# A two-layer encoder trunk on one core: the layer loop is written out in every engine's program, and the router's logits are computed in four column groups

## The reference

```python
xn = rms_norm(x, norm1_w[l])
cols = xn @ w_in[l]
attn = mla_branch(...)        # low-rank attention, 16 heads
hy = hyena_branch(...)        # gated long convolutions, by a transform
merged = gates[:, :, 0] * (attn @ w_attn_branch[l]) + gates[:, :, 1] * (hy @ w_hyena_branch[l])
x = x + merged @ w_out[l]
x = x + expert_choice_ffn(rms_norm(x, norm2_w[l]), router_w[l], ...)
```

```python
def expert_choice_ffn(h, router_w, wg, wu, wd):
    C = max(1, EC_CAPACITY_FACTOR * S // N_EXPERTS)              # 32
    aff = jax.nn.softmax((h @ router_w).astype(jnp.float32), axis=-1)
    gate, idx = lax.top_k(jnp.swapaxes(aff, 1, 2), C)            # 32 tokens for each of 16 experts
    ...                                                          # xs: the tokens of each expert
    a = jnp.einsum('becd,edf->becf', xs, wg)
    u = jnp.einsum('becd,edf->becf', xs, wu)
    o = jnp.einsum('becf,efd->becd', jax.nn.silu(a) * u, wd) * gate[..., None]
    ...                                                          # added back to their tokens
```

## Time and profile before

| | us |
|---|---|
| median of three executions | 2113.52 |
| lowest and highest | 2112.22, 2116.02 |
| the profiled execution | 2112.32 |
| span of the profiled execution, first to last instruction | 2110.5 |
| PE busy | 1606.2 (76%) |
| DVE busy | 508.7 (24%) |
| ACT busy | 287.6 (14%) |
| DMA, mean over the span | 305 GB/s read |

### The profile page before, as it was taken

One profiled execution on the slowest core, in us unless ns is written; L12 is line 12 of the kernel. 1 busy time (PEld: TensorE's weight loads), 2 busy tenths in 40 slices (PEclk: granted clock), 3 DMA queues, 4 the chain that ended last, 5 costly groups with the idle time before them and its releaser, 6 DMA issues.

```text
span 2110.5 us, 23405 instructions
## 1 busy us (share of the span) xinstructions
PE 1606.2 (76%) x9552; PEld 909.9 (43%) x9552; DVE 508.7 (24%) x1057; ACT 287.6 (14%) x594; POOL 45.7 (2%) x24
## 2 busy tenths in 40 slices
PE   7999999876466566666689999997865665665665
PEld 4687688432232132232256866884322222321322
DVE  2654541111111111111126545402111111111111
ACT  2233200200000000000022332002000000000000
POOL 0300000000000000000002000000000000000000
PEclk9999999988788888878899999999887887888888
DMA  7522024679999999999945220246899999999997
GB/s 282 195 85 100 1 80 190 245 319 430 435 423 430 430 427 430 432 429 426 426 149 199 80 100 1 80 189 258 341 434 426 426 430 434 423 430 430 427 430 319
DMA packets 36352, 644.83 MB, mean 306 GB/s; under 512 B 3984, under 2 KB 4880, under 8 KB 6160
## 3 DMA queue, kind: packets, MB, share of 16 engines
q1 hardware_dynamic: 35472, 638.84, 72.2%
q10 hardware_dynamic: 768, 4.29, 0.7%
HBM read 642.07 MB, written 1.05 MB: 305 GB/s over the span
## 4 chain that ended last, share of the span: by engine, by line
PE 49%; DMA 42%; issue 4%; DVE 3%; DVEq 1%; SPq 1%; ACT 1%; ACTq 0%
DMA region<-w_down_dram 27%; DMA ring<-w_up_dram 15%; PE ps L695 7%; PE ps L394 7%; PE ps L619 5%; PE ps L461 5%; PE ps L719 3%; PE ps L644 3%; PE ps L552 2%; PE ps L681 2%; PE ps L587 2%; PE ps L577 2%; PE ps L422 2%; PE ps L484 1%; PE ps L439 1%
## 5 line engine op out<-in xcount | busy, mean ns | idle before, releaser
L695 PE MATMUL ps<-ring,uT 128*32 128x384 f32 (+1 forms) x4096 | 437.7, 567 | 296.8 <-DMA ring<-w_gate_dram 147.6
L695 PEld LDWEIGHTS ps<-ring,uT 128*32 128x32 f32 x4096 | 182.9, 130 | 550.6 <-issue 205.6
L719 PE MATMUL ps<-region,uT 128*32 128x512 f32 x1408 | 175.8, 596 | 34.9 <-DVE uT L1266 22.2
L1262 DVE TENSOR_TENSOR uT<-uT,ps 128x256 f32<-128x256 f32 x32 | 13.5, 421 | 699.4 <-PE ps L695 699.4
L394 PE MATMUL ps<-xnT,ring 128*128 128x256 f32 x768 | 178.3, 380 | 4.5 <-DVE uT L942 2.9
L394 PEld LDWEIGHTS ps<-xnT,ring 128*128 128x128 f32 x768 | 140.6, 190 | 24.1 <-DVE uT L942 4.5
L734 PE MATMUL ps<-uT 128*128 128x512 f32 x256 | 124.3, 618 | 28.8 <-ACT uT L926 28.8
L920 ACT ACT_TABLE_LOAD x32 | 41.1, 1283 | 631.3 <-PE ps L695 631.3
L461 PE MATMUL ps<-xnT,ring 128*128 128x256 f32 x512 | 115.0, 380 | 0.0
L719 PEld LDWEIGHTS ps<-region,uT 128*32 128x32 f32 x1408 | 44.5, 109 | 143.9 <-issue 105.3
L1273 DVE TENSOR_TENSOR x<-x,ps 128x512 f32<-128x512 f32 x128 | 87.9, 687 | 64.4 <-PE ps L734 64.4
(11 more groups left out here) (195 smaller groups left out, 1368.1 us busy)
## 6 DMA issues: line engine op xcount, KB each, us to landing
ring<-w_gate_dram SPq DMA_DIRECT2D x64, 2816.0 KB, 28.4
ring<-w_up_dram SPq DMA_DIRECT2D x32, 5632.0 KB, 32.8
region<-w_down_dram SPq DMA_DIRECT2D x64, 2048.0 KB, 30.6
ring<-units_dram SPq DMA_DIRECT2D x34, 2048.0 KB, 8.0
region<-w_down_dram SPq DMA_DIRECT2D x32, 1536.0 KB, 37.2
ring<-w_lat_dram SPq DMA_DIRECT2D x4, 1344.0 KB, 20.6
ring<-w_q_b_dram SPq DMA_DIRECT2D x2, 2304.0 KB, 29.1
region<-filt_dram ACTq DMA_DIRECT2D x4, 512.0 KB, 11.9
```

The source lines that it names most:

```text
L695: m = mm(bank(b, QW[j], rows=CAP, row0=CAP * j), xs[:, i, q * CAP:(q + 1) * CAP], w[:, i, j * FT:j * FT + QW[j]], start=i == 0, stop=i == ...
L719: m = mm(bank(c, rows=CAP, row0=CAP * j), hT[:, b * P + CAP * j:b * P + CAP * (j + 1)], wd[:, CT * b + j, c * 512:(c + 1) * 512], start=b ...
```

## The change

1. `with engine.Fori(0, DEPTH) as L` becomes `for L in range(DEPTH)` on all five engines. The code of a layer now stands twice in each program, `L` is a number when the program is built, and the branch back to the first layer's code is gone. The inner loops stay.
2. The router's weights are padded from 16 to 32 columns for each block. Products 0 to 3 go to partitions 0, 32, 64 and 96 of bank 4, and products 4 to 7 are added to them in the same places. DVE then copies 128 rows in place of 16, and in place of the two transposes PE multiplies with a constant of 128 x 16 that holds a one where the row's number modulo 32 is the column: this transposes and adds the four groups at once.
3. The constants get 16 columns more (1057 KB become 1065 KB) and the layer's small parameters 128 (68 KB become 132 KB). An argument that makes a reserved scratch area smaller leaves the room for them. No transfer uses that area.

```diff
-W_N = DB + DB * E
+EP = 32
+W_N = DB + DB * EP
...
-        lgT = uT_t[0:E, 4096:4096 + S]
+        lgT = uT_t[:, 4096:4096 + S]
...
-            with sp.Fori(0, DEPTH) as L:
+            for L in range(DEPTH):
...
-            with pe.Fori(0, DEPTH) as L:
+            for L in range(DEPTH):
...
-                    m = mm(bank(4, S, rows=E), fvec[:, W_RT + i * E:W_RT + (i + 1) * E], aT[:, i],
-                           start=i == 0, stop=i == DB - 1)
+                    m = mm(bank(4, S, rows=EP, row0=EP * (i % 4)), fvec[:, W_RT + i * EP:W_RT + (i + 1) * EP], aT[:, i],
+                           start=i < 4, stop=i >= 4)
                 m.then_inc(s["lgT_psum"], 1)
...
-                    m = tp(bank(5, E, t * E), lgT[:, t * P:(t + 1) * P], ident[0:E, 0:E])
+                    m = mm(bank(5, E, t * E), lgT[:, t * P:(t + 1) * P], cst[:, C_SUM:C_SUM + E], start=True, stop=True)
...
-                copy(lgT, bank(4, S, rows=E)).then_inc(s["lgT_dve"], 1)
+                copy(lgT, bank(4, S)).then_inc(s["lgT_dve"], 1)
...
+    c[:, C_SUM:C_SUM + E] = np.arange(P)[:, None] % EP == np.arange(E)[None]
...
+    router = np.pad(k_major(a["router_w"]), ((0, 0), (0, 0), (0, 0), (0, EP - E)))
...
-    nc = bacc.Bacc("TRN2", target_bir_lowering=False, num_devices=1)
+    nc = bacc.Bacc("TRN2", target_bir_lowering=False, num_devices=1, dynamic_dma_scratch_size=2048)
```

More of the change, by code:

```diff
@@ L75 @@
 C_EPS = C_FEAT + S
-C_N = C_EPS + 1
+C_SUM = C_EPS + 1
+C_N = C_SUM + E
 KSC = QR + KVR
@@ L311, in _ @@
         def _(pool):
-            with pool.Fori(0, DEPTH) as L:
+            for L in range(DEPTH):
                 pool.wait_ge(s["qkw_scaled"], L + 1)
@@ L756, in _ @@
                 act.sem_inc(s[n], FREE)
-            with act.Fori(0, DEPTH) as L:
+            for L in range(DEPTH):
                 load_sqrt_table()
@@ L976, in _ @@
             dve.sem_inc(s["x_dve"], X_FREE)
-            with dve.Fori(0, DEPTH) as L:
+            for L in range(DEPTH):
                 dve.wait_ge(s["norm1_rms"], L + 1)
@@ L1337 @@
                            cols(a["filt_skip"].reshape(DEPTH, -1)), small], 2)
-    fvecs = np.concatenate([cols(a["norm2_w"]), k_major(a["router_w"]).reshape(DEPTH, P, -1)], 2)
+    router = np.pad(k_major(a["router_w"]), ((0, 0), (0, 0), (0, 0), (0, EP - E)))
+    fvecs = np.concatenate([cols(a["norm2_w"]), router.reshape(DEPTH, P, -1)], 2)
     qkw = np.concatenate([a["q_norm_w"], a["k_norm_w"]], 1)
```

## The result

The changed kernel takes 2096.7 us (median of six runs, 2094.92 to 2099.73) where the kernel before took 2112.87 us beside it (2109.29 to 2116.02). The ratio is 0.9926, with a 95% interval of 0.9915 to 0.9937: 16 us or 0.7% less. The forecast was 2107.7 us with 2103.8 to 2111.2 us; it was right in the direction and more than 7 us short at the nearer end. The profiled execution took 2094.92 us, its span is 2093.1 us, 17.4 us shorter than before.

The account below looks back on a forecast made before the run. The experts' weight stream sets the pace, so only savings before expert 1's first load count, once per layer. 2.6 + 2.8 + 0.2 + 0.2 = 5.8 us off 2112.32 gave 2106.5, as median 2107.7 us; range 2103.8 to 2111.2.

Parts of the forecast that it names:

- What bounds the kernel: Whole layer: time saved before expert 1's first gate load comes off the end; time saved after it is hidden by DMA.
- The router: Router's products, copy and sum in each layer: exponent 1.37 us sooner, taken as 1.3 us per layer, 2.6 us in all.
- DVE's gap: Second layer's start, L980: DVE waits for instructions after the layer loop's branch back; writing it out saves 2.8 us once.
- the first rival: Second layer's start: DVE's stall stays because code is fetched only when asked for; 2110.5 us, no measurable change; chance 0.16.
- the one with ACT's stalls: ACT's program, fetched piece by piece, stalls some 5.2 us each; two stalls give 2118.1 us, slower; chance 0.06.
- Registers: ACT's three transfers before the second layer's sum: without register instructions between them, 0.2 us off once (0 to 0.3).
- the other 0.2 us: Register work in other places, done while engines wait or have queued work: 0.2 us for the rest, between 0 and 2.
- The 10.8 us of fetching at each branch back of PE: PE's loop over expert groups: 10.8 us of instruction fetching at each branch back stay, hidden by a DMA share of 1.00.
- a DMA share below 1.00: Sign: a share below 1.00 from expert 1 on would make the reading of what is hidden fall.
- The other one: Sign that the forecast is right: time from expert 1's first load to the layer's end is unchanged.
- The third rival: Second layer's first transform products, 7.11 against 5.42 us: small shifts avoid half clock, 1.7 us more gained, 2105.6 us; chance 0.08.

## Why the prediction was right in part and wrong in the sum

**What bounds the kernel** was read rightly: what came sooner ahead of expert 1's gate load came off the end, and the run with PE late by 11 us in the stream shows that PE has room behind it.

**The router**, 2.6 us: right in the profile, where it gave 0.6 and 1.9 us and not 1.3 twice, and near it by medians. The second four products start 1.53 us after the first (forecast 1.54). They and the sum take 0.64 and 0.59 us, not 0.49 and 0.48, so the exponent comes 3.88 us after the first product and not 3.61; what follows made that up, and the gather is 1.37 us sooner, as forecast. PE's granted clock took some back in the first layer, where the gather's products needed 6.72 us at 0.55 on average (before 6.03 us at 0.61), and gave some in the second (5.47 us at 0.69, before 6.19 us at 0.60). By medians the router's part is 2.2 us with both loops at slot 0; with the layer loops kept it was at most 1.9 us.

**DVE's gap**, 2.8 us: right, both ways. It went from 2.84 to 0.03 us, and came back as 2.86 us with DVE's loop alone. The second layer did not pay for instructions behind full queues, so the first rival is out; so is the one with ACT's stalls, of which no run has any. **Registers**, 0.2 us: right. ACT's wait ahead of the second layer's sum is 3.29 us and was 3.45. For the other 0.2 us no run shows anything.

**"The 10.8 us of fetching at each branch back of PE stay, and are hidden: the DMA share over that stretch is 1.00."** This is the step that failed, twice. They don't stay: whether the loop is fetched anew depends on where its head lies (94 packets from slot 224, 40 from slot 0), and the layer loop written out moved the head. And they are not hidden. It is true that PE's standing still is hidden (11 us of it in a group left the streams at 568.70 and 568.78 us), but not the traffic. A DMA share of 1.00 says that the engines are taken, and in these runs further packets in that stretch were a cost and not free: 0.30 to 0.46 MB took 3.0 to 4.5 us of a stream. The prediction said that a DMA share below 1.00 would show this reading wrong; it read 1.01, so that sign could not have shown it. The other one, that the time from expert 1's load on is unchanged, did: 573.65 became 568.75 us. By the runs with the place alone this term is 8 to 10 us: 0.996 of before in one direction (8.4 us), 0.9926 against 0.9973 in the other (9.9 us).

**The third rival**, half the clock at the second layer's first transform products, came true beside the forecast. PE's granted clock was 0.50 from 1253.5 to 1255 us before, and is 1.00 over all of these products now. The changed kernel needs 5.42 us there, not 7.11:

```profile
1242.62 5.42 PE L554 MATMUL ps<-work,consts 128*128 128x512 f32 x12 [0.73 <-DVE work L1110]
```

The wait ahead of it is shorter because the decay table, for which DVE waits, is in use 4.9 us after its issue and not 6.0. In the eight cases with the layer loops kept (four runs, two layers each) that takes 5.5 to 6.2 us, in 23 of the 28 with them written out 4.8 to 5.0, in the other five 5.1 to 6.3. With DVE's gap, 2.8 us, these, 1.1 and 1.7 us, make up the 5.5 us between the streams of this pair of profiles. They are not in every run: where the loops were kept, the half clock came in the second layer once, in the first twice and once in neither, and it came once with them written out (the run with GpSimd's loop, first layer). So for the layer loop DVE's gap and the sum by medians are shown, the division of the rest is not. I had given the half clock a chance of 0.08 as an alternative; it was no alternative but a further term. The run with the loop's place alone and the one with the layer loop and slot 0 too (2103.5 and 2098.1 us, on two chips) differ by 5.4 us, much the same.

The sum as the runs have it: place 8.4, layer loop 5.4, router 2.2, together 16.0 us. The terms come from runs on different chips and are good to a microsecond or two.

Three things stay open: why 0.46 MB of further traffic costs 3 to 5 us of the stream and not 1.1, why fetching the loop anew once (9 packets) and twice (18) costs the first stream 3.0 and 3.2 us but three times only 4.9, and what in the layer loops makes the decay table land later, mostly by 0.9 us. No run puts back the loop of any engine but DVE, so it is not known which one's it is.

## What to carry to other kernels

The stage with a DMA share of 1.00 hid what an engine did (PE 11 us late in a group, streams unchanged), not what the DMA did (0.46 MB more, 3.0 to 4.5 us): count every packet in such a stage, those of the instruction queues too. Before and after any edit ahead of a long loop compare the packets of each instruction queue; if they jump, or gaps marked "issue" stand at the branch back, put the loop's head on the start of a block (96 packets became 42 here) or give its branch a hint (41) before judging the edit. And if a change moves such a loop, measure the change with the loop's place held, as the router could only be told with both at slot 0.

## What the runs showed of the hardware

- A loop of some 1600 PE instructions cost 96 or 94 packets of 16 KB at one place and 39 to 42 at another, in the same kernel. Each time that it was fetched anew PE stood still for 6.5 to 12.0 us.
- At a place between, the same program was fetched anew in some executions only: 2094 or 2100 to 2103 us, 57 packets in the profile of the slower kind and 39 in one of the faster. By the count in blocks of 256 instructions (259 to a packet in the run with the groups written out), the loop was not fetched anew from slot 0, where it lies in seven blocks (40 packets), and was at each branch back from slot 224, where it lies in eight (94).
- With PE's groups written out its gaps were at most 2.0 us, and 36 more packets than with slot 0 (76 and 40) took 6.6 us of the two streams together.
- PE's granted clock fell to 0.50 in the first transform products after 1.86 us of idle PE (7.11 us, before) and 1.91 us (7.12 us, the kernel before with slot 0, first layer), and in the first layers of the runs with the hint on the kernel before and with GpSimd's loop after 2.00 and 2.14 us (7.11 us both), and not where there were 0.60 to 1.70 us (5.42 us).
